# RWKV rounds with sigmoids as tangents on the exponentials' table, and the head norms' inverse roots by Newton steps on GpSimd

## The reference

```python
w_raw = (w0 + jnp.tanh(xw @ w1) @ w2).astype(f32)
w_log = -jax.nn.softplus(-w_raw) - 0.5
decay = jnp.exp(-jnp.exp(w_log))
a = jax.nn.sigmoid(a0 + (xa @ a1) @ a2)
kk = heads(k * k_k)
kk = kk / jnp.maximum(jnp.sqrt(jnp.sum(kk * kk, axis=-1, keepdims=True)), 1e-12)
k = k * (1.0 + (a - 1.0) * k_a)
...
y = _rwkv7_scan(r_h, decay, k_h, v_h, -kk, kk * a_h)
var = jnp.mean(jnp.square(y - mu), axis=-1, keepdims=True)
y = (y - mu) * lax.rsqrt(var + GN_EPS)
```

## Time and profile before

| what | before |
|---|---|
| time, median of 3 runs | 2002.97 us (2002.87 to 2002.98) |
| span of the profiled execution | 2000.4 us (the page gives no other time of it) |
| PE busy | 1942.5 us, 97% |
| DVE busy | 1042.2 us, 52% |
| ACT busy | 798.0 us, 40% |
| POOL busy | 173.0 us, 9%, 191 instructions |
| chain that ended last | PE 86%, DVE 6%, ACT 4%, issue 3% |

### The profile page before, as it was taken

One profiled execution on the slowest core, in us unless ns is written; L12 is line 12 of the kernel. 1 busy time (PEld: TensorE's weight loads), 2 busy tenths in 40 slices (PEclk: granted clock), 3 DMA queues, 4 the chain that ended last, 5 costly groups with the idle time before them and its releaser, 6 DMA issues.

```text
span 2000.4 us, 35450 instructions
## 1 busy us (share of the span) xinstructions
PE 1942.5 (97%) x14631; PEld 1573.8 (79%) x14631; DVE 1042.2 (52%) x1525; ACT 798.0 (40%) x1217; POOL 173.0 (9%) x191
## 2 busy tenths in 40 slices
PE   6999999999999999999989999999999999999999
PEld 5777778888887677777778788888867887888887
DVE  6788765555324745777754544332165465443312
ACT  4345243333224545776634333222254443223322
POOL 1100000000014000000001111111100001111010
PEclk8999999999999999999999999999999999999999
DMA  9545223333332232000013233343222223333331
GB/s 319 179 137 148 85 74 94 98 100 112 102 91 74 63 90 83 11 11 8 9 43 89 85 94 94 94 119 95 71 74 74 85 84 95 94 95 103 111 101 43
DMA packets 313905, 181.62 MB, mean 91 GB/s; under 512 B 18717, under 2 KB 306611, under 8 KB 313780
## 3 DMA queue, kind: packets, MB, share of 16 engines
q1 hardware_dynamic: 308354, 162.82, 27.5%
q0 software_dynamic: 4608, 16.78, 2.6%
q10 hardware_dynamic: 818, 0.21, 0.0%
HBM read 177.69 MB, written 2.10 MB: 90 GB/s over the span
## 4 chain that ended last, share of the span: by engine, by line
PE 86%; DVE 6%; ACT 4%; issue 3%; ACTq 1%; POOL 0%; DVEq 0%; POOLq 0%
PE bank L261 23%; PE bank L262 23%; PE bank L263 23%; PE bank L2409 3%; PE bank L2944 1%; DVE wlo L246 1%; PE bank L1333 1%; PE bank L1335 1%; PE bank L1334 1%; PE bank L612 1%; PE bank L3054 1%; PE bank L2950 0%; ACTq L807 0%; ACT whi L239 0%; PE bank L2971 0%
## 5 line engine op out<-in xcount | busy, mean ns | idle before, releaser
L246 DVE TENSOR_TENSOR wlo<-raw,whi 128x1024 fp32r<-128x1024 f32 (+1 forms) x251 | 327.1, 1303 | 646.2 <-ACT whi L239 646.2
L239 ACT ACTIVATE whi<-raw 128x1024 fp32r<-128x1024 f32 (+1 forms) x251 | 280.6, 1119 | 638.1 <-PE bank L263 631.4
L261 PE MATMUL bank<-fh_hi,whi 128*128 128x512 f32 x991 | 387.0, 391 | 4.9 <-DVE wlo L246 3.3
L262 PE MATMUL bank<-fh_lo,whi 128*128 128x512 f32 x991 | 385.6, 389 | 0.0
L263 PE MATMUL bank<-fh_hi,wlo 128*128 128x512 f32 x991 | 385.5, 389 | 0.0
L261 PEld LDWEIGHTS bank<-fh_hi,whi 128*128 128x128 f32 x991 | 186.0, 188 | 46.3 <-DVE wlo L246 4.4
L262 PEld LDWEIGHTS bank<-fh_lo,whi 128*128 128x128 f32 x991 | 186.0, 188 | 38.8 <-issue 0.5
L263 PEld LDWEIGHTS bank<-fh_hi,wlo 128*128 128x128 f32 x991 | 186.0, 188 | 38.5
L261 PE MATMUL bank<-f_hi,whi 128*128 128x512 f32 x528 | 205.7, 390 | 0.0
L263 PE MATMUL bank<-f_hi,wlo 128*128 128x512 f32 x528 | 205.4, 389 | 0.0
L262 PE MATMUL bank<-f_lo,whi 128*128 128x512 f32 x528 | 205.4, 389 | 0.0
(11 more groups left out here) (522 smaller groups left out, 3172.0 us busy)
## 6 DMA issues: line engine op xcount, KB each, us to landing
raw<-in_w_up_dram SPq DMA_DIRECT2D x44, 512.0 KB, 3.6
raw<-in_ffn_w_gate_dram SPq DMA_DIRECT2D x44, 512.0 KB, 3.6
raw<-in_ffn_w_up_dram SPq DMA_DIRECT2D x44, 512.0 KB, 3.6
raw<-in_ffn_w_down_dram SPq DMA_DIRECT2D x32, 704.0 KB, 4.4
late<-in_ada_w_dram POOLq DMA_DIRECT2D x32, 512.0 KB, 4.3
raw<-in_rwkv_w_rkv_dram SPq DMA_DIRECT2D x24, 512.0 KB, 3.7
raw<-in_w_down_dram SPq DMA_DIRECT2D x16, 704.0 KB, 4.4
early<-in_ada_w_dram SPq DMA_DIRECT2D x16, 512.0 KB, 14.2
```

Of the source, the lines that this page charges most:

```text
L239: act.activation(halves_of(at)[0][:, 0:kts * P], raw_unit(at, kts), ACT.Copy).then_inc(hi_ready, 1)
L246: dve.tensor_tensor(lo[:, 0:kts * P], raw_unit(at, kts), hi[:, 0:kts * P].bitcast(F32), ALU.subtract)\
L261: pe.matmul(dst, hi, rhs_hi(k), start=first and k == 0, stop=False)
L262: pe.matmul(dst, hi, rhs_lo(k), start=False, stop=False)
```

## The change

- **Sigmoids.** sigmoid(x) is 0.5 + 0.5 tanh(x/2). ACT evaluates Tanh with scale 0.5, in the table that the exponentials use; w0 and a0 are halved once at the start (`dve_consts`). For the decay a second ACT pass makes sg out of the tangent. For a the tangent t itself is kept: the factors (1 + t) and 0.5 go into DVE's passes for B (`dve_b`) and into k_a, which is halved.
- **Roots.** The sums are taken over in one pass of 2x4 columns. A second DVE pass reads the float's bits as an integer and writes a first guess of the inverse root. POOL improves it by a cubic and a Newton step (`pool_root`), ten dependent passes on 128x8, and then spreads it by a copy 128x512. PE's turns wait for POOL's `spread` step. The variance's 1/64 goes into the scale of the square on ACT.
- **ACT** loses the two roots, the table-load pass and the table loads, and gains one pass. **DVE** loses two reciprocals and two spreads.
- Waits that were for `sg` are for `a`, and the last gate product counts on another semaphore.

Core of the diff:

```diff
+    def pool_root(pool, turn, s, y):
+
+        POOLn.done(pool.tensor_tensor(root_a, s, y, ALU.mult), "sy")
+        POOLn.wait(pool, turn, "sy")
+        POOLn.done(pool.tensor_tensor(root_b, root_a, y, ALU.mult), "syy")
+        POOLn.wait(pool, turn, "syy")
+        POOLn.done(pool.tensor_scalar(root_c, root_b, 0.375, -1.25, ALU.mult, ALU.add), "c0")
+        POOLn.wait(pool, turn, "c0")
+        POOLn.done(pool.tensor_tensor(root_c, root_c, root_b, ALU.mult), "c1")
+        POOLn.wait(pool, turn, "c1")
+        POOLn.done(pool.tensor_scalar(root_c, root_c, 1.875, None, ALU.add), "c2")
+        POOLn.wait(pool, turn, "c2")
+        POOLn.done(pool.tensor_tensor(y, y, root_c, ALU.mult), "cubic")
+
+        POOLn.wait(pool, turn, "cubic")
+        POOLn.done(pool.tensor_tensor(root_a, s, y, ALU.mult), "ry")
+        POOLn.wait(pool, turn, "ry")
+        POOLn.done(pool.tensor_tensor(root_b, root_a, y, ALU.mult), "ryy")
+        POOLn.wait(pool, turn, "ryy")
+        POOLn.done(pool.tensor_scalar(root_b, root_b, -0.5, 1.5, ALU.mult, ALU.add), "q0")
+        POOLn.wait(pool, turn, "q0")
+        POOLn.done(pool.tensor_tensor(y, y, root_b, ALU.mult), "root")
+        POOLn.wait(pool, turn, "root")
+
+    def pool_kk_root(pool, x_):
+        DVEa.wait(pool, x_, "guess")
+        pool_root(pool, kk_turn(x_), nk_sb[:, :], nk_root)
+        DVEa.wait(pool, x_, "E")
+        POOLn.done(pool.tensor_copy(by_head(sg), over_head(nk_root)), "spread")
+
+    def pool_post_root(pool, j):
+        DVEc.wait(pool, j, "guess")
+        pool_root(pool, post_turn(j), ng_sb[:, :], ng_root)
+        POOLn.done(pool.tensor_copy(by_head(d2), over_head(ng_root)), "spread")
+
     def pool_blocks(pool):
+        pool_kk_root(pool, 0)
         REGION_FREE(pool)
         pool.wait_ge(rkv_ready, 3 * KD)
         eye_of_pair = over_pair(eye2[:, :])
...
+        def body(j, n, x_, y_):
+            if x_ is not None:
+                pool_kk_root(pool, x_)
+            if j is not None:
+                pool_post_root(pool, j)
+
...
@@ -2487,14 +2537,18 @@
         ACTc.done(act.activation(lg_hi[:, :], lg[:, 0, :], ACT.Copy), "lg")
         ACTc.done(act.activation(lg_rest[0:N_REST, :], lg[0:N_REST, 1, :], ACT.Copy), "rest")
 
+    def act_th(act, y_):
+        PEl.wait(act, y_, "lora")
+        DVEa.wait(act, y_, "kkn", before=1)
+        ACTs.done(act.activation(sg, bank[RUN_BANK[0]][:, :], ACT.Tanh, bias=vcol("w0", y_), scale=0.5), "th")
+
     def act_a(act, y_):
-        PEl.wait(act, y_, "lora")
         DVEa.wait(act, y_, "t2", before=1)
-        ACTs.done(act.activation(a_, bank[RUN_BANK[1]][:, :], ACT.Sigmoid, bias=vcol("a0", y_)), "a")
+        ACTs.done(act.activation(a_, bank[RUN_BANK[1]][:, :], ACT.Tanh, bias=vcol("a0", y_), scale=0.5), "a")
 
     def act_sg(act, y_):
-        DVEa.wait(act, y_, "BT", before=1)
-        ACTs.done(act.activation(sg, bank[RUN_BANK[0]][:, :], ACT.Sigmoid, bias=vcol("w0", y_)), "sg")
+        ACTs.wait(act, y_, "th")
+        ACTs.done(act.activation(sg, sg, ACT.Identity, scale=0.5, bias=half_col[:, 0:1]), "sg")
 
     def act_ka(act, y_):
...
     def dve_kk_square(dve, x_):
         PEa.wait(dve, x_, "kk_sum")
-        for e in range(2):
-            DVEa.done(dve.tensor_scalar(of_head(nk_sb, e), sums_of(RUN_BANK[e], 0, NT), 1e-24, None, ALU.max), f"nk{e}")
+        DVEa.done(dve.tensor_scalar(of_heads(nk_sb), sums_of_pair(RUN_BANK[0]), 1e-24, None, ALU.max), "nk")
+        DVEa.wait(dve, x_, "nk")
+        DVEa.done(dve.tensor_scalar(nk_root.bitcast(I32), nk_sb[:, :].bitcast(I32), -0.5, GUESS, ALU.mult, ALU.add), "guess")
 
...
-    def dve_kk_rstd(dve, x_):
-        ACTa.wait(dve, x_, "root")
-        DVEa.done(dve.reciprocal(nk_sb[:, :], nk_sb[:, :]), "rn")
-        DVEa.wait(dve, x_, "rn")
-        DVEa.done(dve.tensor_copy(by_head(sg), over_head(nk_sb)), "spread")
-
...
     def dve_b(dve, x_):
         DVEa.wait(dve, x_, "kkn")
-        DVEa.done(dve.tensor_tensor(sg, kk, a_, ALU.mult), "t2")
+        DVEa.done(dve.scalar_tensor_tensor(B_t[:, :], a_, 1.0, kk, ALU.add, ALU.mult), "t2")
         DVEa.wait(dve, x_, "t2")
-        DVEa.done(dve.tensor_tensor(B_t[:, :], sg, eN, ALU.mult), "BT")
+        DVEa.done(dve.scalar_tensor_tensor(B_t[:, :], B_t[:, :], 0.5, eN, ALU.mult, ALU.mult), "BT")
...
     def dve_post_var(dve, j):
         PEc.wait(dve, j, "var")
-        for e in range(2):
-            DVEc.done(dve.tensor_scalar(of_head(ng_sb, e), sums_of(Y_BANK[e], 0, NT), 1.0 / HD, GN_EPS, ALU.mult, ALU.add),
-                      f"gvar{e}")
-
-    def dve_post_rstd(dve, j):
-        ACTc.wait(dve, j, "root")
-        DVEc.done(dve.reciprocal(ng_sb[:, :], ng_sb[:, :]), "grstd")
-        DVEc.wait(dve, j, "grstd")
-        DVEc.done(dve.tensor_copy(by_head(d2), over_head(ng_sb)), "spread")
+        DVEc.done(dve.tensor_scalar(of_heads(ng_sb), sums_of_pair(Y_BANK[0]), GN_EPS, None, ALU.add), "gvar")
+        DVEc.wait(dve, j, "gvar")
+        DVEc.done(dve.tensor_scalar(ng_root.bitcast(I32), ng_sb[:, :].bitcast(I32), -0.5, GUESS, ALU.mult, ALU.add), "guess")
...
     def pe_kk_spread(pe, x_, n, j):
-        DVEa.wait(pe, x_, "spread")
+        POOLn.wait(pe, kk_turn(x_), "spread")
...
     def pe_post_spread(pe, j):
-        DVEc.wait(pe, j, "spread")
+        POOLn.wait(pe, post_turn(j), "spread")
         PEc.done(pe_turn(pe, POST_BANK, lambda t: d2[:, t * P:(t + 1) * P]), "bc")
```

More of the change, by code:

```diff
@@ L2302, in build @@
     ACTr = Steps("act_run", "xau0 xau1 y0 y1")
-    ACTc = Steps("act_post", "lg rest d2 root")
-    DVEa = Steps("dve_pre", "scan E kp nk0 nk1 bon RT rn spread kkn ends t2 BT AT bonus KT")
+    ACTc = Steps("act_post", "lg rest d2")
+    DVEa = Steps("dve_pre", "scan E kp nk guess bon RT kkn ends t2 BT AT bonus KT")
     DVEm = Steps("dve_inverse", "mt x0 rb " + " ".join(f"z{b}" for b in LEVELS[:-1]) + " z32_0 z32_1")
@@ L2307, in build @@
     DVEr = Steps("dve_run", "hp0 gt1 hp1 gt0 S2 rh1 rh0 " + " ".join(f"S{c}" for c in range(3, NCH)))
-    DVEc = Steps("dve_post", "lg rest gvar0 gvar1 grstd spread yn yb y")
+    DVEc = Steps("dve_post", "lg rest gvar guess yn yb y")
+    POOLn = Steps("pool_roots", "sy syy c0 c1 c2 cubic ry ryy q0 root spread")
+    kk_turn = lambda x_: max(x_, 2 * x_ - 2)
+    post_turn = lambda j: min(2 * j + 3, j + KD)
+    half_col = eps_col[:, 30:31]
+    nk_root, ng_root = cent2[:, CH:CH + 2 * NT], cent2[:, CH + 2 * NT:CH + 4 * NT]
+    root_a, root_b, root_c = (eps_col[:, n:n + 2 * NT] for n in (4, 12, 20))
+    GUESS = float(0x5F3759DF)
     sg, a_, kk = tmp[:, 0, :], tmp[:, 1, :], tmp[:, 2, :]
@@ L2473, in act_exp_e @@
         ACTa.done(act.activation(E_t[:, :], E_t[:, :], ACT.Exp, scale=DECAY), "eE")
-    def act_pre_root(act, x_):
-        DVEa.wait(act, x_, "nk1")
-        ACTa.done(act.activation(nk_sb[:, :], nk_sb[:, :], ACT.Sqrt), "root")
     def act_split_low(act, y_):
@@ L2547, in act_post_square @@
         PEc.wait(act, j, "bc", before=1)
[L2548 removed]
+        ACTc.done(act.activation(d2, y_sb[:, :], ACT.Square, scale=HD ** -0.5), "d2")
     def act_split_y(act, j):
@@ L2552, in act_split_y @@
         act.activation(ys_hi[:, j, :], rkv[:, j, :], ACT.Copy).then_inc(ys_hi_ready, 1)
-    def act_post_root(act, j):
-        DVEc.wait(act, j, "gvar1")
-        ACTc.done(act.activation(ng_sb[:, :], ng_sb[:, :], ACT.Sqrt), "root")
-    def sigmoid_table(act):
-        act.activation(eps_col[:, 1:2], eps_col[:, 0:1], ACT.Sigmoid)
     def act_blocks(act):
@@ L2812, in dve_post_gate @@
         else:
-            dve.wait_ge(last_gate, 1)
+            PEl.wait(dve, KD, "lora")
         DVEc.wait(dve, j, "yb")
@@ L2876, in body @@
                 dve_z(dve, n, 16)
-            if pre:
-                dve_kk_rstd(dve, x_)
-            if run:
-                dve_post_rstd(dve, j)
             if inv:
@@ L2978, in pe_turn_a @@
         elif j is None:
-            ACTs.wait(pe, n + 1, "sg")
+            ACTs.wait(pe, n + 1, "a")
         else:
@@ L2996, in pe_turn_k @@
         if x_ is not None:
-            DVEa.wait(pe, x_, "nk1")
+            DVEa.wait(pe, x_, "nk")
         else:
@@ L3079, in pe_xau @@
         if j + 2 < KD:
-            ACTs.wait(pe, j + 2, "sg")
+            ACTs.wait(pe, j + 2, "a")
         PEr.done(products(pe, [(bank[RUN_BANK[e]][hr[p_], t * P:(t + 1) * P], XT[hr[p_ ^ e], t, e, :],
@@ L3318, in pe_first @@
         if o == 4:
-            ACTs.wait(pe, 0, "sg")
+            ACTs.wait(pe, 0, "a")
             pe_kk_sum(pe, 0, None, None)
@@ L3324, in pe_first @@
             pe_bonus(pe, 0)
-            DVEa.wait(pe, 0, "nk1")
+            DVEa.wait(pe, 0, "nk")
             pe_low(pe, 1)
```

43 lines of the change are left out of this document (20 added, 23 removed).

## The result

The changed kernel takes 2021.06 us (median of 4 runs, 2019.23 to 2022.56) where the kernel before takes 2002.97 (2002.87 to 2003.57): a ratio of 1.0090, 95% interval 1.0075 to 1.0105. It is 15 to 21 us slower. The forecast was 2017.0, in a range of 2005 to 2031, with the step that makes the difference in TensorE's wait ahead of its turn of var.

A forecast was written before the change was run, and what follows sets the result against it. TensorE bounds, so waits for GpSimd's chains are paid in full: 11.0 (six rounds) + 1.1 (round 6) + 2.4 (last block) - 0.5 (first round) = 14.0 us on 2002.97, forecast 2017.0 us, range 2005 to 2031.

The forecast's parts named there:

- What bounds, and the step that decides: TensorE, busy 97% of the span, bounds; GpSimd's two root chains per round decide, making PE stall 1.83 us at var.
- The link: One dependent 128x8 GpSimd pass of a root's ten, duration plus hand-over: taken as 0.27 us, between 0.17 and 0.67.
- The stall: PE's turn of var in a steady round comes 1.83 us later, at 877.55 instead of 875.72; 11.0 us over six rounds.
- The contention at the chain's start: Start of kk's chain beside VectorE's bon and RT passes, two SBUF inputs each: two links slowed, 0.5 us lost.
- kk's turn: PE's turn of kk's spread roots: wanted at 875.23, GpSimd ready at 874.13, so no wait up to 0.37 us per link.
- Round 6: Round j=6 has only the variance's chain; PE already waited there for an X copy, so the cost is 1.1 us.
- the prediction's own last sign of being wrong: The stall at var followed by shorter waits elsewhere in the round, above all at PE's breaks put down to issue; no size.
- Last block: Round j=7: var's spread ends at 1041.50 where PE wanted it at 1039.09; 2.4 us, which the output projection cannot cover.
- Table loads: Three ScalarE loads of 1.28 us and three small activations leave each steady round; counted as 0 gain.
- The gain of round -1: First round, where the exponentials' load delays PE's level 4 products: 0.5 us gained, between 0.3 and 1.5.
- ACT's and DVE's passes: ScalarE's added decay pass, some 0.6 us, fits into 0.73 us of idling; VectorE gets about 0.8 us freer per round; both 0.
- dear-links rival: GpSimd's small two-input passes cost 0.35 to 0.45 us, or contention slows most; 29 us at 0.38, so 2032; chance 0.16.

The follow-up runs named there:

- e2_move: Changed kernel with PE's turn of var put behind level 32, u, the XT turn and the low-rank products, except in the last block; 2007.39 us, 1.0021 of before.
- e3_short: Changed kernel without the last four of each root's ten links (the second Newton step), so roots are approximate; 2003.40 us, 1.0009 of before.
- e1_sig: Changed kernel with both roots back on ScalarE and VectorE, tangents and joined eight-column passes kept; 2001.13 us, 0.9993 of before.
- e8_table: e5_kkpool plus one small ScalarE activation that loads the square root's table at its old place, behind the level 8 X copy; 2002.36 us, 0.9994 of before.
- e7_last: e2_move with the last block's root of the variance on ScalarE and VectorE as before, all other roots on GpSimd; 2003.61 us, 1.0000 of before.
- e5_kkpool: Changed kernel with only kk's root on GpSimd, the variance's root back on ScalarE and VectorE; 2009.90 us, 1.0034 of before.
- e10_long: Changed kernel with four more links in each root (second Newton step done twice); 2049.31 us, 1.0235 of before.
- e6_varpool: Changed kernel with only the variance's root on GpSimd, kk's root back on ScalarE and VectorE; 2017.72 us, 1.0073 of before.
- e9_vartab: e6_varpool with the small Tanh activation put behind ScalarE's X copy of level 16, to load the table earlier; 2011.61 us, 1.0053 of before.
- after_again: The changed kernel unaltered, run once more on the chip of the experiments; 2019.53 us, 1.0084 of before.

## Why the prediction was right, and where its sizes were off

- **What bounds, and the step that decides.** Right. PE waits ahead of var, released by GpSimd's copy, and the wait is paid in full: taking it away by order (e2_move), by length (e3_short) or by engine (e1_sig) gives the rounds' length back to within 0.2 us.
- **The link.** Predicted 0.27 us, measured 0.286. By the prediction's own formula, 20p - 3.57, the stall becomes 2.15 in place of 1.83, and its sum 16.2 us in place of 14.0. This is the largest error. A pass with two inputs on 8 columns takes 0.203 us, 0.02 more than the fixed part worked out for a copy, and the next starts some 0.08 behind its end, where the memsets had 0.06. The prediction's other estimate, 0.29 a link and some 17 us, was nearer in both.
- **The stall.** The 1.83 us are between two starts of the turn of var, so 2.28 is the measure to set beside them, and 2.11 only the idle part. Beyond the link, the contention at the start of kk's chain (next point) is in it: 2.15 + 0.26 = 2.41. The variance's chain then starts 0.57 us behind the start of kk's copy, 0.15 less than assumed. Six rounds: predicted 11.0, measured 13.4.
- **The contention at the chain's start.** Predicted 0.5 us. Measured 0.76: two links take 1.33 where two undisturbed ones take 0.57. The same first link takes 0.63 us on kk's sums and 0.20 on the variance's, where no such pass runs, and links beside the select take 0.20. The Trainium skill (SBUF — State Buffer, Who interferes with whom) has a VectorE pass with two SBUF inputs contend with a GpSimd pass that reads SBUF, and one with at most one SBUF input, outside the 2-port modes, not. The trace agrees: 0.53 and 0.63 us beside such passes, 0.20 beside the select.
- **kk's turn.** Predicted hidden up to p = 0.37. Right: no wait in rounds 0 to 5, and e8_table has kk's root on GpSimd for nothing. The set-up's first root came 0.30 us late where I had 0, and kk's turn in round -1 waited 0.21 us.
- **Round 6.** Predicted 1.1 us, measured 0. The wait of 1.51 stands in the trace, but the break of 1.05 us that the kernel before had behind its turn is gone; set apart from that break, the round grew by 1.08, what was predicted. This was the prediction's own last sign of being wrong (shorter waits elsewhere, above all at the breaks put to issue), and for this round it came true. In e3_short, with a wait of 0.36 and a break of 0.67, the round is 23.43.
- **Last block.** Predicted 2.4, measured 2.44 of idle time, and by e2_move against e7_last a price on the time.
- **Table loads.** Predicted 0 in steady rounds. Right, by e1_sig and e2_move, and all loads in the rounds went, where I had left one. The gain of round -1 (0.5) is not shown apart: up to round 0 the account has 0.2, with the 0.30 and 0.21 us of late turns of kk in it. The Trainium skill (ScalarE: Activation LUTs, What ACT_TABLE_LOAD costs) adds a drain to each switch; the rows of e5_kkpool and e8_table show the load's 1.28 us and 0.02 before the next pass, no drain.
- **ACT's and DVE's passes.** Predicted 0. Right, by e1_sig. DVE's busy time in the rounds fell by 0.5 us each, not 0.8.
- **Left out altogether: the clock.** The terms as measured, 13.4 + 0 + 2.4 - 0.2, make 15.6 in place of 14.0; the rest of the 18.1 is within the interval (15 to 21) and the half clock, about 3.1 us in this execution. So the forecast was 4 us low. Two of its errors offset each other in part: the links and the contention were 2.4 us too cheap in the six rounds, and round 6 was charged with 1.1 us that the missing break paid back. That second one is luck. For the dear-links rival the clock would have mattered: at p = 0.38 its 29 us would have brought waits of 4 us, and e10_long shows what those cost on top. As far as e10_long shows it, that rival's 2032 was too low, and the range's upper end with it.

## What to carry to other kernels

Price a chain of small dependent passes by its serial length (links times duration and hand-over, plus the queue in front of it) and set that against the time until the first in-order consumer; here, offloading work from engines that were not the bound gave nothing, and the chain's excess was paid once per round. Look for work that can stand ahead of the consumer before looking for faster links. Where a table load is free, find out what it hides behind: the same 1.28 us cost nothing or 1 us per round by its place, and removing one use of a table moves the load to the next.

## What the hardware showed that was not expected

- After an idle stretch of 3.9 us PE's granted clock was at half in six of six cases, after 2.4 to 2.6 us in four of six (the last block's wait in the changed kernel, e6_varpool and e9_vartab, not in after_again or e2_move; the 2.64 of e10_long), after 2.1 us in one round of six in each of the two profiles of the changed kernel. It was at half behind the 3.6 us of e10_long's last block too. Behind the waits the half clock lasted from about 3 to 9 us. So an idle stretch of 4 us cost up to twice its length: round 3 of e10_long, with 3.91 and 0.4 us of waits, takes 36.92 us where the kernel before takes 28.43. The length of a wait does not decide alone: half clock also came behind breaks of 1.05 and 0.87 us (e8_table) and not behind the same breaks in the kernel before.
- With twelve dummy products of 480 columns ahead of the wait the clock was at 1.00 in all eight places, and the time about 10 us shorter (2049.3 to 2039.5). At waits of 2 us the same trick gave nothing.
- A GpSimd pass on 128x8 takes 0.20 us with one or two inputs, its dependent successor starts 0.08 us after it. Beside a VectorE pass with two SBUF inputs it takes 0.53 to 0.63.
- A break of about 1 us between PE's products, for which the profile names no releaser, was gone in all five traces in which PE had waited 1.5 us or more just ahead of it. In round 6 of the changed kernel that offset about 1 us of the wait.
